# Earlier summing steps in the first projection and an earlier key norm in the recurrent turns of a two-block transformer kernel

## The reference, cut to what matters

```
mod = silu(c) @ w_ada + b_ada                 # 6 x 2048 values for shift, scale, gate
h = modulate(rms_norm(x), shift_m, scale_m)
q_n, k_c, v_c, k_s, v_s, k_w, v_w, g_n, q_m, k_m, v_m = split(h @ w_in)
q, k_c, k_s, k_w = rope(...)                  # rotary embedding, then attention
...
# second block, one of three branches (rwkv7):
kk = k * k_k;  kk = kk / sqrt(sum(kk * kk))   # per head of 64
k = k * (1 + (a - 1) * k_a)
state = state * w - (state @ kk) * (kk * a) + v * k;   y = state @ r
```

## Time and profile before

| | |
|---|---|
| three executions | 3114.11, 3117.64, 3116.6 us, median 3116.6 |
| profiled execution | 3114.11 us, span 3111.3 us, mean granted TensorE clock 0.973 |
| PE busy | 2963.3 us, 95% of the span |
| DVE, ACT, POOL busy | 1690.7, 1275.6, 136.5 us |
| DMA | 596.69 MB, 192 GB/s over the span |
| first projection after its front part | about 173 to 449 us of the span |
| the four recurrent turns | about 1671 to 1864 us |

### The profile page before, as it was taken

The page is one execution under the profiler, slowest core; times in us unless marked ns, Lnnn a source line. Parts: engine busy times, 40 slices in busy tenths (PEclk is TensorE's granted clock), DMA queues, the critical chain, the costliest instruction groups (busy, mean ns, idle before and its releaser), DMA issues.

```text
span 3111.3 us, 50414 instructions
## 1 busy us (share of the span) xinstructions
PE 2963.3 (95%) x22078; PEld 2732.7 (88%) x22078; DVE 1690.7 (54%) x1484; ACT 1275.6 (41%) x1195; POOL 136.5 (4%) x111
## 2 busy tenths in 40 slices
PE   4899999899999999989999889999998999999998
PEld 4899987899889997789998779999978998899887
DVE  6868877784444444454445754334645444444444
ACT  2234444444334443345343444443334443344433
POOL 0011110000000000000012410000000000000000
PEclk8898999999999999999999999999999999999999
DMA  9998767595555555545451015556554555555553
GB/s 354 342 322 283 259 236 281 189 354 191 189 188 180 186 181 178 194 159 166 150 172 40 7 49 182 177 188 204 176 173 136 179 188 185 186 186 181 177 184 122
DMA packets 300434, 596.69 MB, mean 192 GB/s; under 512 B 12128, under 2 KB 17760, under 8 KB 299744
## 3 DMA queue, kind: packets, MB, share of 16 engines
q1 hardware_dynamic: 298976, 590.12, 56.8%
q10 hardware_dynamic: 1280, 3.93, 0.5%
HBM read 583.80 MB, written 6.29 MB: 190 GB/s over the span
## 4 chain that ended last, share of the span: by engine, by line
PE 83%; DVE 8%; ACT 4%; DMA 2%; issue 2%; POOL 1%; SPq 0%; DVEq 0%; ACTq 0%
PE ps L2209 32%; PE ps L2168 25%; PE ps L2687 10%; PE ps L2321 3%; PE ps L2306 2%; DMA ada<-w_ada 2%; DVE ada_acc L1442 2%; PE ps L2806 2%; PE ps L2282 2%; DVE wL L1284 2%; ACT wH L750 1%; PE ps L2571 1%; PE ps L2248 1%; PE ps L2186 1%; ACT probs L944 1%
## 5 line engine op out<-in xcount | busy, mean ns | idle before, releaser
L1284 DVE TENSOR_TENSOR wL<-raw,wH 128x2048 fp32r<-128x2048 f32 x436 | 1004.9, 2305 | 1210.9 <-ACT wH L750 1210.0
L750 ACT ACTIVATE wH<-raw 128x2048 fp32r<-128x2048 f32 x436 | 834.8, 1915 | 1353.1 <-PE ps L2209 546.9
L2209 PE MATMUL ps<-actH,wH 128*128 128x256 f32 x2816 | 799.2, 284 | 6.4 <-DVE wL L1284 6.4
L2209 PE MATMUL ps<-actL,wH 128*128 128x256 f32 x2816 | 797.6, 283 | 0.0
L2209 PE MATMUL ps<-actH,wL 128*128 128x256 f32 x2816 | 797.5, 283 | 0.0
L2209 PEld LDWEIGHTS ps<-actH,wH 128*128 128x128 f32 x2816 | 541.3, 192 | 8.1 <-issue 4.1
L2209 PEld LDWEIGHTS ps<-actL,wH 128*128 128x128 f32 x2816 | 541.4, 192 | 0.3 <-issue 0.2
L2209 PEld LDWEIGHTS ps<-actH,wL 128*128 128x128 f32 x2816 | 541.3, 192 | 0.0
L2168 PE MATMUL ps<-wH,hidH 128*128 128x512 f32 x1024 | 406.9, 397 | 1.2 <-DVE wL L1284 1.2
L2168 PE MATMUL ps<-wH,hidL 128*128 128x512 f32 x1024 | 405.9, 396 | 0.0
L2168 PE MATMUL ps<-wL,hidH 128*128 128x512 f32 x1024 | 405.9, 396 | 0.0
(11 more groups left out here) (404 smaller groups left out, 3666.0 us busy)
## 6 DMA issues: line engine op xcount, KB each, us to landing
raw<-w_in SPq DMA_DIRECT2D x96, 1024.0 KB, 5.2
ada<-w_ada SPq DMA_DIRECT2D x80, 1024.0 KB, 8.8
raw<-w_up SPq DMA_DIRECT2D x64, 1024.0 KB, 5.3
raw<-w_down SPq DMA_DIRECT2D x64, 1024.0 KB, 5.1
raw<-w_mlp_up SPq DMA_DIRECT2D x64, 1024.0 KB, 5.2
raw<-w_mlp_down SPq DMA_DIRECT2D x64, 1024.0 KB, 5.0
raw<-w_gates SPq DMA_DIRECT2D x48, 1024.0 KB, 5.1
raw<-w_o SPq DMA_DIRECT2D x16, 1024.0 KB, 5.8
```

Source lines behind the costliest of these rows:

```text
L750: nc.scalar.activation(wH[:, s % SPLIT if L[name]["spg"] > 1 else r % SPLIT, :, :], raw[:, slot, :, :], ACT.Copy).then_inc(wh_ready, 1)
L1284: nc.vector.tensor_tensor(wL[:, b, :, :], raw[:, slot, :, :], wH[:, b, :, :].bitcast(F32), ALU.subtract).then_inc(wl_ready, 1)
L2209: ins = nc.tensor.matmul(out, w[:, b, k, cols], v[:, kk, :], start=(kk == 0 and j == 0 and n % 2 == 0), stop=(kk == STEP_K * spg - 1 and j ...
```

## The change

It has two independent parts, and nothing is added or left out: the same instructions stand in another order.

In the first projection DVE's list for groups 0 and 1 is rewritten, and the first two rows of `WIN_ADA` with it, so that SP asks for the `w_ada` blocks to match.

```
-    WIN_ADA = [(0, 0, 0, 2), (2, 1, 3, 4)] + [(1, 1, 0, 2)] * 6
+    WIN_ADA = [(0, 1, 0, 1), (2, 3, 1, 4)] + [(1, 1, 0, 2)] * 6
             compress_inputs()
+            rope(1)
+            ada_blocks(1)
             split("w_in", 0, 0, 2)
-            rope_sin(1)
-            rope_sum(1)
             split("w_in", 0, 0, 3)
-            ada_blocks(2)
+            ada_blocks(1)
 
             split("w_in", 0, 1, 0)
             ada_blocks(2)
+            rope(2)
             split("w_in", 0, 1, 1)
-            rope_sin(2)
+            ada_blocks(3)
+            split("w_in", 0, 1, 2)
             ada_blocks(1)
-            rope_sum(2)
-            split("w_in", 0, 1, 2)
-            ada_blocks(3)
             modulation(8, 3)
```

## The result

| | before | after |
|---|---|---|
| executions on one chip, in turns | median 3116.6 us of five (3113.9 to 3128.49) | median 3150.73 us of five (3146.18 to 3156.25) |
| profiled execution, its span | 3114.11, 3111.3 us | 3151.21, 3149.4 us |
| mean granted TensorE clock | 0.973 | 0.960 |

The changed kernel takes 1.0104 of the time before (95% interval 1.0081 to 1.0128), 34 us more. I had forecast 3130 (3119 to 3137): slower was right, and the size was less than half of the one measured.

What follows compares the result with a forecast made beforehand. It took PE, busy 95% of the span, as the bound, not the summing work. To 3114.1 us it added 14.0 for the projection (5.3 + 6.2 + 5.4 - 2.9) and 2 for the turns: 3130, range 3119 to 3137.

Steps and rivals of the forecast that it cites:

- Group 0's stall: First projection, step (0, 2): PE waits 5.3 us for DVE's split(0, 2), bounds 3.1 and 7.6.
- Rival 2: First projection: POOL takes 5.75 us in both rotary units, or the swap is later still; 3134.7 us, chance 0.11.
- Group 1's stall: First projection, step (1, 1): PE waits 6.2 us for split(1, 1) behind rotary unit 2, bounds 3.7 and 8.5.
- rival 3: First projection, group 1: the swap of rotary unit 2 lands in 6.5 us; 3127.6 us, chance 0.07.
- The clock behind the two waits: First projection: a lower clock costs 2.7 us behind each new wait, 5.4 in all, bounds 0 and 5.4.
- The wait of 2.88 us gone: First projection, step (2, 0): PE's old wait for DVE goes, giving back 2.9 us.
- rival 6: First projection: summing work is the bound, so the 2.88 us wait and its slow step go; 3108.5 us, chance 0.04.
- Rival 4: First projection: stalls are handed back later as PE's other waits for `wL`, 5.7 us, vanish; 3124.4 us, chance 0.08.
- The recurrent turns: Recurrent turns: reciprocals ahead of level 5's Ym start the first chunk later; three turns lose 2 us in sum.
- So turn 1 loses 1.2 ... Sum +2. Bounds: -4 ... and +5: Recurrent turns: turn 1 loses 1.2 us, turn 0 about 0, turn 2 0.5 to 1; sum +2, bounds -4 and +5.
- `unit_keys` out of chunk 1: Recurrent turns, chunk 1: `unit_keys` leaves it, where the next state update waits behind it; 0.65 us back.

Runs made afterwards that it cites:

- e8: e1 plus unused PE products, four ahead of step (0, 2) and three ahead of step (1, 1) of the first projection; 1.0025 of the kernel before.
- e12: The whole changed kernel plus 1, 3 and 3 unused PE products in the waits for level 5's Ym in turns 0 to 2; 1.0014 of the kernel before.
- e7b: The kernel before with only group 1 of the first projection in the new order; 0.9996 of the kernel before.
- experiment 6: Unused PE products put into the two new waits of the first projection, with the turns as before (e8); 1.0025 of the kernel before.
- e2: The kernel before with only the edits in the recurrent turns; 1.0062 of the kernel before, median 3138.8 us.
- e5: e2 plus 1, 3 and 3 unused PE products in the waits for level 5's Ym in turns 0 to 2; 0.9984, median 3113.5 us.
- e1: The kernel before with only the edits in the first projection, turns as before; 1.0017 of the kernel before.
- e13: e9 plus two unused products in the 2.88 us wait ahead of step (2, 0) of the first projection; 0.9979 of the kernel before.
- e3: The kernel before with only PE's and ACT's edits in the turns, DVE's list as before; 0.9992 of the kernel before.
- e6: The kernel before with only group 0 of the first projection in the new order; 1.0024 of the kernel before.
- e10: The kernel before, nothing moved, plus unused PE products: three at level 3 of turn 0, one ahead of turns 0 to 2's first chunk; 0.9965, median 3108.2 us.
- e9: e3 plus unused PE products: three at level 3 of turn 0, one ahead of the first chunk in turns 0 to 2; 0.9977 of the kernel before.

## Why the prediction was right in sign and wrong in size

**Group 0's stall: right.** 5.14 us against 5.3, POOL at 3.46 against 3.44, split(0, 2) at 188.90 against 188.4. Rival 2 (POOL at 5.75) fell. In e8 and e12 POOL took 2.65 and 2.51 us and DVE's sine product 3.38 and 3.37 instead of 1.2; the sum started 3.8 and 3.6 us behind POOL's start, as in the changed kernel (3.6).

**Group 1's stall: 4.17 against 6.2,** inside its bounds. The term that was too large is the swap: ACT issued it at 206.58 and it landed at 214.6, 8 us where I had kept the 10 of before. That is rival 3 in part. It follows from group 0's new order: with it POOL started 8.1 to 8.6 us behind the swap's issue in five traces and 9.3 in e8; with group 0 as before 9.1 to 10.4, and in e7b, with 9.9, the wait was 5.93. Which load made room is not shown.

**The clock behind the two waits: right for group 0, in part luck for group 1.** Steps (0, 2) and (0, 3) take 14.25 us for 11.75 [+2.5], step (1, 1) 8.65 for 6.00 [+2.65], against 2.7 each; the granted clocks were 0.80 and 0.65, not near half. e8's 6.00 us shows that work in the wait can keep step (1, 1) fast. But the same step was slow without any wait in five other traces (experiment 6), so the 6.00 us of the kernel before that I took as its price were its best case.

**The wait of 2.88 us gone: right, and counted too small.** The slow step behind it was part of the same thing. With the wait the fall of the clock goes too, and step (2, 0) takes 5.99 us for 8.65. I had put these 2.7 us into rival 6 and not into my own sum. With them: 5.14 + 2.5 + 4.17 + 2.65 - 2.88 - 2.66 = 8.9 of the 9.3 us that the projection adds by step (3, 0). What is left is the balance of small terms: step (1, 2) is 1.2 us longer, the small products behind it 1.0 and step (1, 3) 0.6 shorter, steps (2, 1) and (2, 2) 0.5 longer. Both the wait and the slow step behind it differ from one execution to the next: with the same lists the wait was 0.52 us in e2 and 5.07 in e5, and the step took 5.98 to 8.65.

**Rival 4, handed back later: no.** The distance at step (3, 0) stays to the end of the projection. Instead w_o costs about 5 us in this execution, in a wait that I had not looked at. It differs from run to run: 3.39 us in the changed kernel, 2.66 in e12, 1.52 in e1, and, with DVE's projection lists of before, 1.80 in e13 and 4.12 in e3. So this load is late by chance more than by the change.

**Rival 6, the summing work as the bound: no.** Both waits stand. (Its 3108.5 leaves out the 2 us of the turns; with them it is 3110.5.) But e8's and e6's waits ahead of step (2, 0) show that DVE is close behind PE there: up to that point no more than about 1 to 2 us can be won on PE alone.

**The recurrent turns: here the prediction failed.** The step that failed is the term "So turn 1 loses 1.2 ... Sum +2. Bounds: -4 ... and +5". Its waits were nearly right. Turn 1's wait for `Ym` grew by 2.26 us (I had 1.8). The wait of 2.48 at level 3 went, but ACT's `key_squares` brought one of 1.69 ahead of `key_sums`, so 0.8 was won. Turn 2 lost as much in waits as turn 1, although DVE had been idle there for 2.08 us ahead of `Ym`. I had read that idle time as slack, and it was PE's own slowness: the levels of turn 2 ran at a granted clock of 0.85 before, those of turn 1 at 1.00. In the changed kernel both turns' levels run at 1.00, so DVE has the same time in both. Before, turns 1 and 2, then after, the same levels:

```profile
1740.00:1750.00 10.00, 9.62 (x242) 8.23 (x242) 8.99 (x16) 6.31 (x15) 0.00 (x0) 1.00 0.01 2
1789.00:1800.60 11.60, 11.18 (x242) 9.74 (x242) 9.07 (x16) 6.36 (x16) 0.00 (x0) 0.85 0.01 3
```

```profile
1764.00:1773.50 9.50, 9.35 (x242) 7.93 (x240) 8.63 (x15) 5.92 (x14) 0.00 (x0) 1.00 0.02 3
1820.00:1829.60 9.60, 9.45 (x242) 8.00 (x241) 8.73 (x15) 6.02 (x14) 0.00 (x0) 1.00 0.01 2
```

The waits make about 1.5 us in each of turns 1 and 2 and 0.3 in turn 0. What is missing is 21 us, and it is the clock. I had priced it in the projection and left it out in the turns, though the earlier trace rows had the fall behind a wait of 3.92 us of turn 0, and I had forecast a first chunk that starts 1.8 us later behind an idle PE. I had also taken the fall as a fixed price, 2.7 us, the length that it had in front of dense 128x256 products. In the chunks PE runs products of 64x64 with short waits between, and the clock did not come back in 18 to 26 us. The runs show 25 us for three turns (e2 against e5) and 28 us (the ratios of the changed kernel and of e12), 8 to 9 a turn. One term of the turns was right: `unit_keys` out of chunk 1 gives 0.65 back. At a clock of 1.00 the chunks take 28.4 us with DVE's new list (e5, e12) and 29.1 with the old one.

The Trainium skill (TensorE: Matmul & The Clock Gate, Part 1) says that the throttled state is the default and activity releases it. In the turns the traces agree for the fall: it came behind idle PE, and not where products filled the wait. For the release they do not bear the sentence out as it stands: in turn 0 of the changed kernel PE was busy for 21.41 of 22.00 us and the clock stayed at 0.50 throughout. Busy time as the profile counts it was not enough here, and the measurement decides.

**Of the time as a whole.** The forecast of 3130 was made on a profiled execution of 3114.1. e1 and e12 show what the change was worth without the turns' clock: 1.0017 and 1.0014, 4 to 5 us, where the traces of both show 9.2 to 9.3 us in the projection alone. Why the times show less is open. The intervals reach 9 to 10 us, and single traces differ too: from the end of step (0, 1) to step (3, 0) the lists of before took 100.3 to 104.1 us in seven traces, the new ones 111.8 to 112.0 in three. The kernel before has executions from 3105 to 3133 us. e10 shows that idle PE in the turns is part of the reason: with products in these waits the range is 3102.7 to 3111.8, and a long fall in one turn, as e1, e6 and e8 have it, is worth 9.5 us (38.6 for 29.1).

## What to carry to other kernels

Price a wait of TensorE by what stands behind it. Ahead of dense wide products, waits of 2.7 to 5.9 us cost 1.5 to 2.7 us more in slow matmuls (steps (0, 2) and (2, 0)). Ahead of the chunks, a chain of small products, a long fall cost 8 to 11 us: it came in 3 of 21 turns behind a wait of 1.1 us, and in all 4 behind 3.4 us. So, when an edit on another engine lengthens such a wait by 2 us, look up the granted clock in the rows of the stretch behind it, in more than one execution, since a single trace may show its best case. Where the wait can't be avoided, unused products in a free bank are a cheap cure to try (they helped in the turns, and e8 shows no gain in the projection), and adding them is also a clean test of whether the clock is the cause.

## What the runs showed that was not expected

- The lower clock can last through 22 us in which PE is 97% busy (stretch 1722 to 1744 of the changed kernel), when what it runs are small products. It can do so behind the old wait of 1.10 us too (e1, e6, e8), only more rarely.
- The same wait does not always throw the clock: 1.68 us in turn 0 threw it in the changed kernel's profiled execution and not in e2's. This can spread the times of one kernel by 10 us a fall. Products in the waits narrowed e3's 3106 to 3128 to e9's 3106 to 3111, apart from two.
- The same POOL product of 128x1024 took 5.31 to 5.75 us in four kernels with group 0 as before, beside a split and a sine product on DVE, and 3.38 to 3.46 us beside the sine product alone in most traces. In the other four with group 0 as before (e2, e3, e7b, e13) it took 2.40 to 2.50 us, and DVE's split 4.38 to 4.54 instead of 2.28. So either engine can be the one that pays, and 3.44 us was not its undisturbed time. An estimate from these rows: 2.4 plus the split's 2.28 and the sine product's 1.22 is 5.9, as if they ran one after the other.
